# Moving two adaLN row steps, one normalisation step and one cast in a fused three-block transformer kernel

## The reference

```python
# first block: branch A ends in a normalisation per head
ya = rms_norm(diff_attention(...), subln_gain, 1e-5) * (1 - lam_init)
# every one of the 12 modulation vectors (6 of each block): a row times a 1024x1024 weight
ada = silu(c) @ ada_w + ada_b          # shift, scale, gate of mixer and of feed-forward
# block 0: neighbourhood attention beside a gated linear recurrence, whose output is gated, then projected
x = x + gate * (concat(na, hgrn2) @ ev_w_out);   x = x + gate * ffn(modulate(norm(x)))
# block 1: gated short convolution, then feed-forward
b, c, u = split(h @ od_w_in);  y = b * dwconv3(c * u);  x = x + gate * (y @ od_w_out)
x = x + gate * ffn(modulate(norm(x)));   out = norm(x)
```

## Time and profile before

| | |
|---|---|
| median of 3 runs | 1072.67 us (1072.22 to 1074.28) |
| profiled execution, its time | 1072.67 us |
| its span, first to last instruction | 1070.9 us |
| PE busy | 1047.8 us (98%) |
| DVE busy | 779.3 us (73%) |
| ACT busy | 580.6 us (54%) |
| DMA, mean | 206 GB/s |

### The profile page before, as it was taken

The page is one execution under the profiler, slowest core; times in us unless marked ns, Lnnn a source line. Parts: engine busy times, 40 slices in busy tenths (PEclk is TensorE's granted clock), DMA queues, the critical chain, the costliest instruction groups (busy, mean ns, idle before and its releaser), DMA issues.

```text
span 1070.9 us, 21438 instructions
## 1 busy us (share of the span) xinstructions
PE 1047.8 (98%) x9048; PEld 1000.2 (93%) x9048; DVE 779.3 (73%) x1128; ACT 580.6 (54%) x880; POOL 63.7 (6%) x77
## 2 busy tenths in 40 slices
PE   8999999999999999999899999999999999999997
PEld 8989889999999999897688999999899989999996
DVE  6367778765576768987877999967687769677642
ACT  5556665565445665534656655543544447565432
POOL 2000000000010614000100000000010010000000
PEclk9999999999999999999999999999999999999999
DMA  9557657565755674444657888767768666555621
GB/s 282 174 184 253 227 168 213 182 197 181 241 168 163 193 219 158 137 140 164 212 167 247 275 294 278 268 251 289 266 210 289 216 213 209 186 180 183 231 79 40
DMA packets 165917, 220.30 MB, mean 206 GB/s; under 512 B 4498, under 2 KB 146222, under 8 KB 165821
## 3 DMA queue, kind: packets, MB, share of 16 engines
q1 hardware_dynamic: 164442, 215.67, 61.5%
q0 software_dynamic: 832, 1.65, 0.8%
q10 hardware_dynamic: 546, 1.60, 0.4%
HBM read 217.80 MB, written 1.11 MB: 204 GB/s over the span
## 4 chain that ended last, share of the span: by engine, by line
PE 80%; DVE 12%; ACT 3%; DMA 2%; issue 2%; SPq 0%; DVEq 0%; ACTq 0%
PE psG L562 19%; PE psG L564 18%; PE psG L563 18%; PE psS L562 4%; PE psS L564 4%; PE psS L563 4%; DVE wlo L1811 4%; DVE arow L1875 1%; DMA raw<-in_w_in_dram 1%; PE psG L705 1%; PE psG L678 1%; PE psG L680 1%; PE psG L691 1%; DMA raw<-in_ada_w_dram 1%; PE psS L836 1%
## 5 line engine op out<-in xcount | busy, mean ns | idle before, releaser
L1811 DVE TENSOR_TENSOR wlo<-raw,whi 128x1024 fp32r<-128x1024 f32 x311 | 375.7, 1245 | 101.8 <-ACT whi L1229 96.0
L562 PE MATMUL psG<-Hlo,whi 128*128 128x256 f32 x1424 | 405.9, 285 | 1.5 <-DVE Hlo L1840 0.8
L564 PE MATMUL psG<-Hhi,whi 128*128 128x256 f32 x1424 | 401.4, 282 | 0.0
L563 PE MATMUL psG<-Hhi,wlo 128*128 128x256 f32 x1424 | 401.1, 282 | 0.0
L1229 ACT CAST whi<-raw 128x1024 fp32r<-128x1024 f32 x311 | 314.2, 1048 | 121.3 <-PE psS L564 32.2
L562 PEld LDWEIGHTS psG<-Hlo,whi 128*128 128x128 f32 x1424 | 269.1, 189 | 5.6 <-issue 2.6
L563 PEld LDWEIGHTS psG<-Hhi,wlo 128*128 128x128 f32 x1424 | 269.2, 189 | 0.0
L564 PEld LDWEIGHTS psG<-Hhi,whi 128*128 128x128 f32 x1424 | 269.1, 189 | 0.0
L562 PE MATMUL psS<-Glo,whi 128*128 128x256 f32 x352 | 100.1, 284 | 0.1
L564 PE MATMUL psS<-Ghi,whi 128*128 128x256 f32 x352 | 99.3, 282 | 0.0
L563 PE MATMUL psS<-Ghi,wlo 128*128 128x256 f32 x352 | 99.2, 282 | 0.0
(11 more groups left out here) (435 smaller groups left out, 1720.9 us busy)
## 6 DMA issues: line engine op xcount, KB each, us to landing
raw<-in_ada_w_dram SPq DMA_DIRECT2D x48, 1024.0 KB, 5.6
raw<-in_ffn_w_up_dram SPq DMA_DIRECT2D x44, 1024.0 KB, 5.3
raw<-in_w_in_dram SPq DMA_DIRECT2D x29, 1024.0 KB, 6.4
raw<-in_ev_w_in_dram SPq DMA_DIRECT2D x26, 1024.0 KB, 5.4
raw<-in_ffn_w_down_dram SPq DMA_DIRECT2D x22, 1024.0 KB, 4.9
raw<-in_od_w_in_dram SPq DMA_DIRECT2D x12, 1024.0 KB, 8.1
raw<-in_w_in_dram SPq DMA_DIRECT2D x9, 512.0 KB, 6.7
raw<-in_w_o_dram SPq DMA_DIRECT2D x4, 1024.0 KB, 5.2
```

The lines of the kernel that those rows point to most:

```text
L562: mm(o, a_hi, b_lo, start=first, stop=False, skip_group_check=shared)
L563: mm(o, a_lo, b_hi, start=False, stop=False, skip_group_check=shared)
L564: return mm(o, a_hi, b_hi, start=False, stop=last, skip_group_check=shared)
L1811: V.tensor_tensor(ring_half(wlo, v, h - H0[v]), src, ring_half(whi, v, h - H0[v]).bitcast(F32), ALU.subtract).then_inc(lo_split, 1)
```

## The change

It has three parts, all of them moves.

1. **Rows 8 and 10.** `spread(8)` moves on PE from the tenth unit of block 0's second feed-forward product (i = 9 of `DOWN_SPREAD`) to the place behind unit b of i = 0 in the odd mixer. `sum_ada(8)` moves there from i = 0 to i = 2, `sum_ada(10)` from i = 1 to i = 3. ACT's `keep_spread(8)` and DVE's `keep_ada` calls move with them. `spread(9)` stays where it was, right behind the loop.
2. **The logarithm in slots 8 and 9** (line 1402) moves on ACT behind the casts of the next unit (`ahead`), the copy of branch output (`keep_y`) and, in the code of slot 7, the square.
3. **The cast of `lg`** becomes one instruction of 128x1024 in step 3 in place of two of 128x512 in steps 2 and 3; step 2's wait for `sub_taken` goes.

```diff
--- before.py
+++ after.py
@@ -469,7 +469,7 @@
         NA = 8
         EVO_AT = {5: 0, 6: 1, 7: 2, 8: 3}
         UP_SUMS, UP_SPREAD = ({6: 5, 10: 6}, {2: 11}), ({5: 5, 9: 6}, {})
-        DOWN_SUMS, DOWN_SPREAD = ({6: 7}, {}), ({4: 7, 9: 8}, {})
+        DOWN_SUMS, DOWN_SPREAD = ({6: 7}, {}), ({4: 7}, {})
         SUM_IX = {n: i for i, n in enumerate(ADA_ORDER)}
         FOLDS = [n for n in ADA_ORDER if n not in ON_VECTOR]
         ADDED = {n: 4 * i + 4 for i, n in enumerate(ON_VECTOR)}
@@ -1185,8 +1185,10 @@
                     project_pair(uc, uu, "mix1")
                 project(ub, Hhi, Hlo)
                 if i == 0:
+                    spread(8)
+                elif i == 2:
                     sum_ada(8)
-                elif i == 1:
+                elif i == 3:
                     sum_ada(10)
             spread(9)
             for n, u in enumerate(SPAN["odo"]):
@@ -1397,16 +1399,16 @@
                 nc.scalar.copy(Mhi[:, 4 * b:4 * b + 4, :], sg[:, 4 * b:4 * b + 4, :]).then_inc(M_high, 1)
 
             for s, fill in enumerate(SLOT):
+                ahead(fill[0])
+                if s >= 3:
+                    keep_y(s - 3)
+                if s == 7:
+                    nc.scalar.activation(sqv[:, 0:4, :], yA[:, :, :], ACT.Square).then_inc(sub_sq, 1)
                 if s in (8, 9):
                     act.wait_ge(sub_sum, s - 7)
                     nc.scalar.activation(headr[:, s - 8, :], psX[:, :], ACT.Ln, bias=eps[:, 1:2], scale=1.0 / P
                                          ).then_inc(sub_taken, 1)
                     act.wait_ge(sub_taken, s - 7)
-                ahead(fill[0])
-                if s >= 3:
-                    keep_y(s - 3)
-                if s == 7:
-                    nc.scalar.activation(sqv[:, 0:4, :], yA[:, :, :], ACT.Square).then_inc(sub_sq, 1)
                 if s == 9:
                     nc.scalar.activation(headr[:, :, :], headr[:, :, :], ACT.Exp, scale=-0.5).then_inc(sub_inv, 1)
                 if s >= 2:
@@ -1666,12 +1668,9 @@
                     step(square_output(3))
                     step(nc.scalar.activation(lbc[:, 1, :], lbc[:, 0, :], ACT.Ln, bias=eps[:, 0:1], scale=1.0 / P))
                     nc.scalar.activation(lbc[:, 2, :], lbc[:, 1, :], ACT.Exp, scale=-0.5).then_inc(sub_inv, 1)
-                elif s == 2:
-                    act.wait_ge(sub_taken, 3)
-                    nc.scalar.copy(Hhi[:, 4:6, :], lg[:, 0, 0:2, :])
                 elif s == 3:
                     act.wait_ge(hg_gated, 2)
-                    nc.scalar.copy(Hhi[:, 6:8, :], lg[:, 0, 2:4, :]).then_inc(hg_high, 1)
+                    nc.scalar.copy(Hhi[:, 4:8, :], lg[:, 0, :, :]).then_inc(hg_high, 1)
                 keep_rows(f"na{s}a")
                 if s >= 2:
                     keep_turned(s - 2, 1)
@@ -1759,6 +1758,8 @@
                 act.wait_ge(cu_set, i + 1)
                 conv_centre(fa[:, i % 2, :, :], n, C_ODW + 8 + 2 * i, C_ODB + 2 * i, fz[:, i % 2, :, :])
                 ahead(ub)
+                if i == 1:
+                    keep_spread(8)
             for n, u in enumerate(SPAN["odo"]):
                 if n == 0:
                     keep_spread(9)
@@ -2432,9 +2433,9 @@
                 then(V.tensor_tensor(z, z, bank(ub).rearrange("p (a b) -> p a b", a=2), ALU.mult),
                      bank_free[B0[ub] % 2], B0[ub] // 2 + 1)
                 split_value(z, Ghi[:, 2 * i:2 * i + 2, :], Glo[:, 2 * i:2 * i + 2, :], G_ready, n + 1)
-                if i == 0:
+                if i == 2:
                     keep_ada(SUM_IX[8] + 1)
-                elif i == 1:
+                elif i == 3:
                     keep_ada(SUM_IX[10] + 1)
             gains(4, 4, C_FFN + 8)
             for n, u in enumerate(SPAN["odo"]):
```

## The result

The changed kernel took 1081.49 us, median of four runs (1080.00 to 1084.49), the kernel before 1072.79 beside it: ratio 1.0083, interval 1.0058 to 1.0106, slower by 8.7 us between these medians where 5.1 were forecast. The time lies over the forecast's range. The profiled execution took 1082.89 us, its span is 1081.2.

The account below looks back on a forecast made before the run. PE, busy 98% of the span, was taken as the bound, so time moves only with its work or standing. Terms 4.2 + 0.9 + 0.0 = +5.1 us on 1072.67 gave 1077.8 us, range 1076.0 to 1080.1.

Parts of the forecast that it names:

- PE's moved work, 0: PE's spread(8), 0.66 us, and sum_ada(8), 0.36 us, are only moved, paid once before and after: 0.
- Term A: PE stands at spread(9) until DVE's keep_ada(10) after i = 3: +4.2 us, bounds +2.8 and +5.2.
- DVE's clock in the new kernel: DVE before spread(9): 0.66 us earlier without spread(8), 0.28 for one fewer keep_ada; keep_ada(10) starts at 845.24.
- nothing absorbs the stall: Behind spread(9), no later wait pays the 4.2 us back, and nothing new comes late.
- a rival with 0.23 and up to 2.1 us: Clock falls during PE's standstill at spread(9): 5.1 + up to 2.1 us, about 1079.5 us; chance 0.23.
- The price of 2.1: Cost of returning from low clock, from the kernel's start: 22 matmuls took 4.82 us where 2.7 was expected.
- the end rows: Behind the last matmuls, PE idle over 4 us, clock 1.00 to 0.50; the 4.3 us standstill was judged close to this.
- Term B: PE's first transposes wait for ACT's later logarithm, +0.74 in slot 8, +0.17 in slot 9: +0.9 us, bounds 0 and +1.4.
- Term C: Merged lg cast in neighbourhood attention, step 3 growing 0.43 us before 0.41 idle: 0.0 us, bounds -0.2 and +0.4.
- The stall was not hidden: Rival: DVE reaches keep_ada(10) before PE reaches spread(9), or PE gets past it; 1073.6 us, chance 0.06.
- nothing got faster: Rival: ACT's freed starts in slots 8, 9 and attention step 2 shrink PE's waits; 1070 us if stall hidden too; chance 0.03.
- B was not absorbed: Rival: the slot 8 and 9 cost is absorbed while the spread(9) stall stands; 1076.9 us, chance 0.08.

Follow-up runs that it names:

- the fold held back: Kernel before with only the row 8 and 10 moves, GpSimd's fold of row 10 waiting until DVE multiplied c and u of i = 2: 1079.32 us, ratio 1.0048.
- the repetition: The whole changed kernel timed once more against the kernel before, nothing else altered: 1082.5 us, ratio 1.0083.
- part 1 alone: Only the moves of rows 8 and 10, made to the kernel before: 1082.1 us, ratio 1.0079.
- part 2 alone: Only the logarithm moved behind the casts in slots 8 and 9, made to the kernel before: 1075.39 us, ratio 1.0018.
- the eleventh experiment: Kernel before plus identity matmuls filling PE's waits in neighbourhood attention, nine in step 5, six in step 2: 1072.96 us, ratio 0.9995; one run 2598.54 us.

## Why the prediction was right or wrong

- **Direction, and PE as the bound: right.** All of the loss is time in which PE stands or runs at half clock.
- **PE's moved work, 0: right.** 0.72 us left one stretch and 0.66 of it came into the next.
- **Term A, +4.2: the mechanism right, the size wrong.** The first step that failed is "DVE's clock in the new kernel", which counted what left DVE's own stream and nothing beside it. Less `spread(8)`, the third stretch grew by 6.41 - 0.72 = 5.7 us, over the bound of 5.2. With the fold held back it is 4.3. I had written that the change moves ACT's copy of row 8 at cost 0, and had named for it PE and ACT, not GpSimd, which waits for its count. A moved increment of a counter moves everyone who waits for a later value.
- **The rest of A.** That nothing absorbs the stall: right, the last stretch is the same to 0.07 us.
- **The clock: the second step that failed, and the larger miss.** The sum has no term for it; it was held for a rival with 0.23 and up to 2.1 us. It fell at the end of the 5.3 us standstill in all three profiles with part 1 as it is (after, the repetition, part 1 alone), and it cost 2.5 to 2.7 us there, which alone carries the forecast's sum (1077.8) over its range (1080.1). Even with the forecast's own wait of 4.29 us it fell and cost 1.4. The price of 2.1 came from 22 warm-up matmuls; the measured one is longer at half clock (6.7 us) on a dense stretch. The likelihood was too low because I took the end rows for the nearest case and did not treat their change from 1.00 to 0.50 behind 4 us as the likely case here. The other row, 1.00 through 2.2 us, showed one of two outcomes of the same wait: in 7 of 13 profiles the clock fell there. What "TensorE: Matmul & The Clock Gate" of the Trainium skill says in "Why this matters for your kernels", that a long idle gap between bursts brings the clock to half, the trace bears out with 5.32 us idle, then 0.50.
- **Term B, +0.9: the right places, 1.3 to 1.4 in size.** By the brackets slot 8 is 0.93 for 0.74 and slot 9 0.36 for 0.17. By PE's starts with part 2 alone, from the scores of slot 8 (L836) to the transposes are 1.86 us for 0.86, and from there to those of slot 9 10.55 for 10.14: 1.0 and 0.4. ACT's casts don't start at the end of the copy but 0.17 us behind it, through a semaphore that the logarithm had covered before; that is most of the 0.2 in each slot. ACT's timeline in slot 8, after:

```profile
127.35 0.37 ACT L1257 COPY arow<-psG 128x256 f32<-128x256 f32 x1 [1.18 <-PE psG L705]
127.89 1.99 ACT L1231 CAST whi<-raw 128x1024 fp32r<-128x1024 f32 x2 [0.17 <-ACT arow L1257]
129.79 0.36 ACT L1391 COPY kaT<-psY 128x256 f32<-128x256 f32 x1
130.19 0.69 ACT L1409 ACTIVATE tok<-psX,eps 128x512 f32<-128x512 f32 x1
```

  Inside the bounds (0 to 1.4), at their upper end. The clock behind it, 1.5 us in the profile of after, had no term and no bound.
- **Term C, 0.0: right.** 1.0001 (0.9992 to 1.0010); the cast took 1.05 us as worked out.
- **The rivals.** The stall was not hidden, nothing got faster, and B was not absorbed (1.0018 for part 2 alone, 1.0009 to 1.0027).

In sum, of the 5.2 us between the forecast's span (1076.0) and the measured one (1081.2): 2.7 are the clock behind `spread(9)`, 1.5 the rest of A (5.7 for 4.2), 0.9 the first stretch (1.8 for 0.9, no more than executions differ there by themselves), 0.1 not assigned. This is one execution; the median of the four lies 1.4 us lower, and the forecast's 1077.8 is 3.7 us under it.

What stays open: the parts' ratios add to 1.0098 where the whole has 1.0083, inside the intervals; how often the clock falls in slot 8; the one long run of the eleventh experiment.

## What to carry to other kernels

When an increment of a counting semaphore moves, list every engine that waits for that value or a later one, and look at what it will then run beside. Before a new wait on the bounding engine, price it twice, as its length and as the clock behind it; if it can't be avoided, let the engine do covered work first, here the unit that needed only part of the late data (1.0007 in place of 1.0079). And compare versions by the distance between landmarks of one engine: it finds 1.4 us in 1073 where the totals of single executions can't. But first look in several executions how much each stretch varies by itself; here the first one varied by 2.9 us and the others hardly.

## What the runs showed of the hardware

- DVE's `SCALAR_TENSOR_TENSOR` of 128x255, two inputs in SBUF, took 0.48 us alone and 1.50 to 1.53 and 0.84 beside a GpSimd `TENSOR_TENSOR`, which itself took 2.24 for 1.29. The times fit engines that take turns: GpSimd's fold began at 808.57 while DVE's split ran; counted back by its 1.29 from its end at 810.81 it really ran from 809.52, about where the split ended (the next DVE instruction begins at 809.59). The addition that began at 809.59 ended 0.28 behind the fold's end (811.09), and the next one 0.28 behind the second fold (811.97 and 811.69).
  "SBUF — State Buffer" of the Trainium skill, section "Who interferes with whom", says that a DVE instruction with two SBUF inputs contends with a GpSimd instruction that reads SBUF, and that the later one blocks until the other is through. The trace agrees, in both directions.
- The granted clock fell from 1.00 to 0.50 while PE still stood, about 0.6 us before the end of the 5.32 us in the profile of after, and in part 1 alone: a window from 848.40 to 848.90 there has no PE work and 0.50. At the waits of 2.2 us it fell about when PE began again or up to 1.2 us later. With standstills of 5.3, 4.3 and 2.2 us it was at half for 6.8, 3.4 and 3.4 us, which cost 2.5 to 2.7, 1.4 and 1.5 to 1.6 us; behind 2.2 us it fell in 7 of 13 profiled executions, and once behind 1.91 us.
- In slot 8 it fell behind 0.93 us of idle time, in a stretch of small matmuls with PE busy for 2.48 of 3.40 us, and did not in two other executions with the same wait.
- A float32 matmul of 128 columns into PSUM left two records on PE and took 0.22 us at full clock, so 20 of them filled 4.4 us.
